# h2 doubled by TensorE instead of by DMA, 128-partition moves of states and index keys, and tile 0 first in the opening

## The chip, the cores and the metric

The kernel runs on one core of one Trainium2 chip. The metric is the device time of one launch in microseconds; the median of several launches is quoted.

## What is computed

One step of a streaming encoder layer on 384 tokens of width 1024: 256 prompt tokens and 8 streams of 16 tokens. It is cut here to what matters.

```python
h = rmsnorm(x, ln1_g); q_a, k_a, v_a, q_i, k_i, w_i, q_b, k_b, v_b, g_b = split(h @ w_in)
score = sum_h w_i * relu(q_i . k_i)          # index scores, masked by chunk
idx = top_k(score)                           # 64 of 128/256 keys, 132 of 528
o_a = softmax(q_a . k[idx]) @ v[idx]         # sparse attention
o_b, S_new = retention(q_b, k_b, v_b, S)     # 4 heads, state (64, 128) each
x = x + concat(o_a, silu(g_b) * norm(o_b)) @ w_out
h2 = rmsnorm(x, ln2_g)
q = h2 @ w_query                             # 8 heads, two halves of 128
i1, i2 = top16(q1 . keys1), top16(q2 . keys2)
e, gate = top16 of the 256 sums; gate = softmax
x = x + sum_{head, 16} gate * gelu(u[e] . h2) * v[e]     # rows of u, v: 16384 x 1024
y = rmsnorm(x, ln_final_g)
```

## The kernel before

The tokens are three tiles of 128: tiles 0 and 1 are the prompt, tile 2 is the 8 streams. Each tile has 8 experts' heads of 16 chosen experts, so there are 24 units (tile, head) and 384 steps n of one gather each. A step n belongs to unit n // 16 and to tile n // 128.

**The expert stream.** GpSimd issues the gathers: step n fetches 128 rows of 8 KB (one expert's u and v for each partition) into one of 8 row buffers, n % 8. VectorE multiplies the u half with the token's h2 and sums; ScalarE applies Gelu, multiplies with the gate and builds a diagonal matrix; TensorE (`add_experts`) takes two steps at a time with 8 matmul records of 512 columns and adds the v halves to the tile's output in PSUM. Gather n + 8 waits for `acc` of step n. Since one gather serves 64 tokens with two experts each, VectorE needs every token's h2 twice: `h2r` holds, for j = 0 and 1, the rows of h2 of half j on both halves of the partitions. In this kernel four DMAs on SyncE's queue (`twice`) copy h2 there for each tile, each from 64 partitions to 64 partitions.

**The work beside the stream.** Each engine has one instruction stream in order. From step 0 on, each engine's program holds the stream's instruction of step n, and after it those parts of the other work whose written time `until(k)` has come: queries and top-16 of the later units, the attention and retention of tiles 1 and 2, their output projections, and the index scores of tile 2. These numbers k are steps.

**The opening.** Before step 0 everything that unit 0 of tile 0 needs has to be done: projections, index scores and top-64, attention, retention, output projection (`x1_done` reaches 2), the norm of h2, its transposes (`h2_t`), the query of unit 0, the scores against the expert keys (`query_scores`), `top16(0)` on VectorE, and `spread_out(0)` with `spread_take(0)`, which raises `picked` and lets the first gather go. In this kernel the opening also holds the index queries, index scores, top-64 and attention scores of tile 1 (`two_tiles`, `sums_1`, `scores_1`, `row_max`, `exps_1`, `scale_probs`), the index queries of tile 2 (`later_qi`) and the attention queries of tiles 1 and 2 (`later_qa`).

**Buffers that order the loads.** The eight row buffers hold weights at first: gathers 0 to 3 go where `w_out` of tile 0 was, gathers 4 and 5 where `w_qi` is and wait for `qi_ps` 3, gathers 6 and 7 where `w_qa` is and wait for `qa_ps` 3. Slot 0 of `wt` (named T) holds tile 1's index queries, weights and scores, and afterwards the query weights `w_q`, of which one quarter (2 MB, two units) is loaded at a time by `load_q(k)` once the units that use the quarter before are done.

**SyncE's queue** issues every other load and store in the order of the program. The states `s0` (1 MB in, 1 MB out) go in two DMAs of 64 partitions each, and the index keys `cki` in eight DMAs of 64 partitions.

Of the kernel before, what the change touches and what calls it, by code (L numbers as in the profile page):

```python
# [19 lines left out]
ALU = mybir.AluOpType  # L20
# [3 lines left out]
P = 128  # L24
D = 1024
KC = D // P
# [4 lines left out]
HI = 8  # L31
# [52 lines left out]
def build(nc, a, o):  # L84
    with ExitStack() as ctx:
# [179 lines left out]
        w_in = {n: sem("w_" + n) for n in ("kv", "qi", "qa", "vb", "qkb", "gb", "out0", "out1", "out")}  # L265
# [7 lines left out]
        h2r_in = [sem(f"h2r_in{t}") for t in range(TILES)]  # L273
# [43 lines left out]
        def q_at(u):  # L317
            return {2: 0, 3: 6, 8: 88, 16: 224, 17: 230}.get(u, 16 * u - 48)
# [40 lines left out]
        def _(sp):  # L359
# [23 lines left out]

            sp.wait_ge(kv_sb, TILES)
# [26 lines left out]
            sp.dma_start(wt[:, 4, :], a["w_out0"]).then_inc(w_in["out"], 16)  # L411
            load_q(3)
            sp.wait_ge(gb_ps, 3)
            sp.dma_start(wt[:, 5, :], a["w_out1"]).then_inc(w_in["out"], 16)
# [12 lines left out]
            for e in range(2):  # L427
                sp.dma_start(s0[64 * e:64 * e + 64, :, :, :], a["s0"][e]).then_inc(s0_in, 16)
# [4 lines left out]
            for e in range(2):  # L433
                sp.dma_start(o["state_s"][e], s0[64 * e:64 * e + 64, :, :, :]).then_inc(ss_out, 16)
# [1397 lines left out]
```

## Time and profile before

| | |
|---|---|
| median of 3 runs | 1257.58 us (1254.51 to 1259.72) |
| profiled execution, its own time | 1257.35 us |
| its span, first to last instruction | 1255.6 us |
| busy: TensorE, VectorE, ScalarE, GpSimd | 900.1, 812.7, 486.1, 436.7 us |
| moved by DMA | 463.92 MB, of it 402.68 MB by the gathers |

The span is what lies between the first and the last instruction; the profiled execution's own time is 1.75 us longer. Busy times of engines overlap, so they don't add up to the span.

### The profile page before, as it was taken

The page shows a single profiled execution, that of the slowest core. Times are in us where ns is not written, and L with a number is a line of the kernel's source. Part 1 is how long each engine was busy: PE and PEld are TensorE (multiplying, and loading weights), DVE is VectorE, ACT ScalarE, POOL GpSimd, SP SyncE. Part 2 cuts the span into 40 slices and gives each one's busy share as a digit, 9 for nine tenths or more (in the row PEclk, how much of TensorE's full clock was granted, in tenths as well). Part 3 has the DMA queues.
Part 4 walks back from the last instruction along what each step waited for, and adds up shares of the span by engine and source line. Part 5 has one row for each costly group of instructions (what it writes and reads, how often), then busy time and mean ns, then how long its engine had stood idle before and what let it go on. Part 6 is the DMA issues. An engine that isn't in the chain of part 4 may idle for free.

```text
span 1255.6 us, 12036 instructions
## 1 busy us (share of the span) xinstructions
PE 900.1 (72%) x3676; PEld 407.6 (32%) x3676; DVE 812.7 (65%) x2103; ACT 486.1 (39%) x1444; POOL 436.7 (35%) x405
## 2 busy tenths in 40 slices
PE   6999787997696875765776786746757777665564
PEld 4855643442233232332333432222222222221110
DVE  2152557585576668998676785836696776677543
ACT  2111234253344443243366664422453443444332
POOL 0000134253244342334443333523444444443440
PEclk9899988899798896978787889878787778777866
DMA  9611479999999999989999999999999999999994
GB/s 381 269 68 34 148 299 424 373 365 424 394 421 365 397 364 421 418 332 420 419 420 420 417 421 422 420 364 422 398 418 389 422 421 422 420 422 417 422 420 164
DMA packets 67793, 463.92 MB, mean 369 GB/s; under 512 B 8720, under 2 KB 10512, under 8 KB 15760
## 3 DMA queue, kind: packets, MB, share of 16 engines
q0 software_dynamic: 55296, 402.68, 78.9%
q1 hardware_dynamic: 12432, 60.47, 12.5%
q8 instruction: 29, 0.48, 0.2%
q14 instruction: 36, 0.29, 0.1%
HBM read 456.73 MB, written 3.24 MB: 366 GB/s over the span
## 4 chain that ended last, share of the span: by engine, by line
DMA 44%; PE 28%; DVE 15%; issue 5%; ACT 4%; POOL 3%; SPq 0%; DVEq 0%; POOLq 0%
DMA rows<-in_uv,ids 43%; PE ps L530 27%; DVE rows L1765 7%; POOL rows L500 3%; ACT work L1088 1%; ACT wgt L1088 1%; DMA wt<-in_w_q 1%; PE ps L533 1%; DVE wt L1377 1%; DVE top L1373 1%; ACT zact L1088 1%; ACT L1088 1%; ACT wt L1088 0%; DMA half<-in_half 0%; DVE work L1486 0%
## 5 line engine op out<-in xcount | busy, mean ns | idle before, releaser
L530 PE MATMUL ps<-rows,work 128*64 128x512 f32 x1536 | 488.1, 768 | 309.5 <-ACT work L1088 309.1
L500 POOL DMA_INDIRECT rows<-in_uv,ids x384 | 418.6, 1090 | 679.2 <-PE ps L530 585.8
L1765 DVE CUSTOM_DVE_ANT_0 rows<-rows,masks 128x1024 f32<-128x1024 f32 x256 | 313.5, 1226 | 196.6 <-DMA rows<-in_uv,ids 194.0
L1088 ACT ACTIVATE zact<-zdot 128x1 f32<-128x1 f32 x384 | 77.5, 202 | 590.0 <-DVE zdot L1765 589.4
L530 PEld LDWEIGHTS ps<-rows,work 128*64 128x64 f32 x1536 | 111.2, 162 | 581.0 <-ACT work L1088 413.1
L1765 DVE CUSTOM_DVE_ANT_0 rows<-rows,wt 128x1024 f32<-128x1024 f32 x128 | 157.1, 1227 | 100.7 <-DMA rows<-in_uv,ids 99.0
L530 PE MATMUL ps<-wt 128*128 128x512 f32 (+4 forms) x476 | 141.5, 442 | 2.9 <-DVE wt L1544 1.9
L1088 ACT ACTIVATE work<-pair,wgt 128x64 f32<-128x64 f32 x384 | 133.5, 348 | 12.5
L530 PEld LDWEIGHTS ps<-work,wt 128*128 128x128 f32 (+1 forms) x776 | 100.0, 204 | 69.1 <-issue 67.9
L530 PE MATMUL ps<-work,wt 128*128 128x128 f32 (+1 forms) x776 | 114.9, 297 | 5.3 <-DMA wt<-in_w_q 4.4
L1088 ACT ACTIVATE wgt<-zact,gates 128x1 f32<-128x1 f32 x384 | 113.1, 295 | 12.5
L530 PEld LDWEIGHTS ps<-wt 128*128 128x128 f32 (+1 forms) x476 | 73.5, 194 | 61.2 <-issue 54.9
L1088 ACT ACT_TABLE_LOAD x66 | 84.7, 1283 | 1.9 <-PEq L1815 0.7
L1088 ACT ACTIVATE wt<-ps 128x512 f32<-128x512 f32 (+5 forms) x59 | 32.2, 555 | 81.2 <-PE ps L530 55.7
L530 PE MATMUL ps<-wt,rows 128*128 128x128 f32 (+1 forms) x320 | 48.0, 314 | 0.0
L530 PEld LDWEIGHTS ps<-wt,rows 128*128 128x128 f32 x320 | 45.1, 209 | 2.7 <-issue 1.0
L1765 DVE DVE_READ_ACCUMULATOR2_ANT zdot<- 128x1 f32 x384 | 31.5, 82 | 0.0
L530 PE MATMUL ps<-wt,work 128*128 128x512 f32 x64 | 30.0, 606 | 0.0
L479 POOL TENSOR_TENSOR rstd<-veps,half 128x4 f32<-128x4 f32 x3 | 4.4, 1456 | 70.1 <-DVE veps L1427 70.0
L475 POOL TENSOR_TENSOR rstd<-ms,half 128x1 f32<-128x1 f32 x9 | 8.4, 928 | 54.9 <-DVE ms L1358 48.6
L1456 DVE MAX8 work<-ps 128x8 f32<-128x128 f32 x48 | 11.9, 290 | 19.7 <-PE ps L530 19.4
L530 PE MATMUL ps<-x,wt 64*128 64x128 f32 (+4 forms) x100 | 22.7, 346 | 2.0 <-DVE x L1552 2.0
(134 smaller groups left out, 608.8 us busy)
## 6 DMA issues: line engine op xcount, KB each, us to landing
wt<-in_w_q SPq DMA_DIRECT2D x10, 2048.0 KB, 12.5
rows<-in_uv,ids POOLq DMA_INDIRECT x384, 13.0
rows<-in_w_out SPq DMA_DIRECT2D x2, 2048.0 KB, 32.3
wt<-in_w_out SPq DMA_DIRECT2D x2, 2048.0 KB, 12.2
wt<-in_ckv SPq DMA_DIRECT2D x16, 256.0 KB, 11.4
x<-in_x SPq DMA_DIRECT2D x5, 512.0 KB, 8.7
rows<-in_w_qi SPq DMA_DIRECT2D x1, 2048.0 KB, 13.2
rows<-in_w_qa SPq DMA_DIRECT2D x1, 2048.0 KB, 15.3
```

The lines of the kernel that those rows point to most:

```text
L475: pool.tensor_tensor(rstd[:, n:n + 1], ms[:, n:n + 1], half4[:, 0:1], ALU.pow).then_inc(rsd, 1)
L479: pool.tensor_tensor(rstd4[:], veps[:], half4[:], ALU.pow).then_inc(o_rstd, 1)
L500: pool.indirect_dma_start(row[s], None, a["uv"], bass.IndirectOffsetOnAxis(ap=ids[:, own(n // KP).start + n % KP:own(n // KP).start + n % ...
L530: return nc.tensor.matmul(out, lhsT, rhs, start=start, stop=stop)
L533: return nc.tensor.transpose(out, in_, ident[0:k, 0:k])
L1088: return nc.scalar.activation(*args, **kw)
L1373: then(V.max(out=top8[:], in_=score))
L1377: then(V.match_replace(out=score, in_to_replace=top8[:], in_values=score, imm_value=TAKEN))
L1456: ins = V.max(out=top[:, e, 0:8], in_=s[e])
L1765: V.tensor_tensor_reduce(row[s][:, 0:D], row[s][:, 0:D], h2r[t % 2][:, n % 2, :], 1.0, 0.0, ALU.mult, ALU.add, zdot[:, s:s + 1]).then_inc( ...
```

## The change

`twice` is no longer a DMA. TensorE multiplies 64 rows of `pair` (a 128 x 128 matrix with a one where the two indices agree modulo 64) with 64 rows of h2, which puts those rows on both halves of the partitions in one PSUM bank; four such matmuls of 512 columns and four ScalarE copies make the `h2r` of a tile. VectorE waits for `h2r_set` in place of the DMA's semaphore. The states move in one DMA over 128 partitions each way, and the index keys in four DMAs over 128 partitions (two streams at a time); ScalarE copies the even streams' index queries to the lower partitions for it.

In the opening, tile 0's index queries go alone, tile 0's scores, retention and output come before everything of tile 1, and the index queries, scores and top-64 of tile 1 follow behind tile 0's query and its `query_scores`. Index queries of tile 2 come before the query of unit 1, the attention queries of tiles 1 and 2 are last. Attention scores, maxima, exponentials and scaling of tile 1 move from the opening to steps 0 to 14, and what follows them of tile 1's attention and retention, and the projections, comes about 2 to 8 steps later. Tile 1's index data moves out of slot 0 of `wt`, so that `load_q(0)` is issued ahead of the cache outputs; `load_q(3)` moves ahead of the `state_p` output and of `w_out`.

The diff is cut; left out are changed step numbers (most of tile 1 later by 2 to 6), bank numbers, and the order of tile 0's pieces on ScalarE.

```diff
-        T = wt[:, 0, :]
...
-        qiT1 = at(T, 0, HI * P).rearrange("p (g h t) -> p g h t", h=HI, t=STEPS)
-        wz1 = at(T, 1024, WZ)
-        relu1 = at(T, 2176, 1024).rearrange("p (b n) -> p b n", b=2)
-        score1 = at(T, 3200, 256)
+        qiT1 = at(B, 7168, HI * P).rearrange("p (g h t) -> p g h t", h=HI, t=STEPS)
+        relu1 = at(B, 5888, 1024).rearrange("p (b n) -> p b n", b=2)
+        score1 = at(B, 6912, 256)
...
+            load_q(0)
...
-            sp.wait_ge(biased, 2)
-            load_q(0)
-
-            def twice(t):
-
-                sp.wait_ge(hready, TILES + t + 1)
-                for j in range(2):
-                    for q in range(2):
-                        sp.dma_start(h2r[t % 2][64 * q:64 * q + 64, j, :], h2[64 * j:64 * j + 64, :]).then_inc(h2r_in[t], 16)
-
-            twice(0)
...
+            load_q(3)
...
-            def load_cki(b):
-                sp.dma_start(cki[64:128, b % 4, :], a["cki"][b]).then_inc(cki_in[b % 4], 16)
-
+            sp.dma_start(wt[:, 5, :], a["w_out1"]).then_inc(w_in["out3"], 16)
             sp.wait_ge(vb_sb, 3)
-            for b in range(4):
-                load_cki(b)
-            twice(1)
-            for b in range(4, STREAMS):
-                sp.wait_ge(dots, CACHE + b - 3)
-                load_cki(b)
+            for b in range(STREAMS // 2):
+                sp.dma_start(cki[:, b, :], a["cki"][2 * b:2 * b + 2].rearrange("e d t -> (e d) t")).then_inc(cki_in[b], 16)
             sp.wait_ge(summed, CACHE + STREAMS)
-            for e in range(2):
-                sp.dma_start(s0[64 * e:64 * e + 64, :, :, :], a["s0"][e]).then_inc(s0_in, 16)
+            sp.dma_start(s0, a["s0"].rearrange("e d q h v -> (e d) q h v")).then_inc(s0_in, 16)
...
-            for e in range(2):
-                sp.dma_start(o["state_s"][e], s0[64 * e:64 * e + 64, :, :, :]).then_inc(ss_out, 16)
+            sp.dma_start(o["state_s"].rearrange("e d q h v -> (e d) q h v"), s0).then_inc(ss_out, 16)
...
-            twice(2)
...
-            pool.memset(wz1, 0.0).then_inc(wz_zero, 1)
...
+            pool.wait_ge(wout, 2)
+            pool.memset(wz, 0.0).then_inc(wz_zero, 1)
...
-            def two_tiles(bank, w, j):
-
-                for t in range(2):
+            def index_queries(t, bank, j0, j1):
+
+                for j in range(j0, j1):
                     for c in range(KC):
-                        last = mm(ps[:, bank, j % 2 * 256 + t * P:j % 2 * 256 + (t + 1) * P], w[:, c, j * P:(j + 1) * P],
-                                  hT(t, c), c == 0, c == KC - 1)
-                return last
+                        last = mm(ps[:, bank, j * P:(j + 1) * P], w_qi[:, c, j * P:(j + 1) * P], hT(t, c), c == 0, c == KC - 1)
+                if j1 == 4:
+                    last.then_inc(qi_ps, 1)
 
             pe.wait_ge(w_in["qi"], 16)
-            for j in range(4):
-                if j % 2 == 0:
-                    pe.wait_ge(kv_sb, 2 + j // 2)
-                last = two_tiles(7 - j // 2, w_qi, j)
-                if j % 2:
-                    last.then_inc(qi_ps, 1)
+            index_queries(0, 4, 0, 4)
...
-            BANK1 = (0, 1, 4, 5)
-            for b in range(4):
-                for g in range(2):
-                    last = mm(ps[:, BANK1[b], g * 256:(g + 1) * 256], qiT1[0:DH, 2 * b + g, :, :], kiw[0:DH, :])
-                last.then_inc(dots, 1)
-            for j in range(2, GRP):
-                last = flipped(ps[:, 7, j * P:(j + 1) * P], w_qa, j, hT0)
-            last.then_inc(qa_ps, 1)
-            pe.wait_ge(wz_set, 2)
-
-            def sums_1(b):
-                pe.wait_ge(relued, DOTS[1] + b + 1)
-                for g in range(2):
-                    i = 2 * b + g
-                    last = mm(ps[:, 2, 0:256], wz1[:, i * P:(i + 1) * P], relu1[:, b % 2, g * 256:(g + 1) * 256], i == 0, i == 7)
-                last.then_inc(summed, 1)
-
-            sums_1(0)
-            sums_1(1)
-            pe.wait_ge(w_in["vb"], 16)
-            natural(0, w_vb, 6, 512, 0, 4)
-            sums_1(2)
-            sums_1(3)
-            natural(0, w_vb, 6, 512, 4, 8).then_inc(vb_ps, 1)
             pe.wait_ge(w_in["qkb"], 16)
...
+            def twice(t, i, bank):
+
+                j, e = divmod(i, 2)
+                r = slice(64 * j, 64 * j + 64)
+                mm(ps[:, bank, :], pair[r, :], h2[r, e * 512:(e + 1) * 512]).then_inc(dup_ps, 1)
...
+            mm(ps[:, 2, 0:P], e8[64:64 + HI, :], kiw[64:64 + HI, P:2 * P]).then_inc(w_ps, 1)
+            index_queries(1, 6, 0, 3)
+            h2_t(0)
+            index_queries(1, 6, 3, 4)
+            query(0)
+            pe.wait_ge(qi_sb, 2)
+            pe.wait_ge(wz_set, 2)
+            dots_1(0)
+            dots_1(1)
+            query_scores(0)
+            pe.wait_ge(gb_sb, 1)
+            dots_1(2)
+            dots_1(3)
+            twice(0, 0, 6)
+            sums_1(0)
+            sums_1(1)
+            twice(0, 1, 1)
+            sums_1(2)
+            sums_1(3)
+            twice(0, 2, 2)
+            twice(0, 3, 0)
+            index_queries(2, 7, 0, 1)
+            spread_out(0)
+            index_queries(2, 7, 1, 4)
+            query(1)
+            query_scores(1)
+            pe.wait_ge(h2r_set, 1)
             later_qa(0)
             later_qa(1)
-            h2_t(0)
-            query(0)
+            pe.wait_ge(qi_sb, 3)
             later_qa(2)
-            query_scores(0)
+            spread_out(1)
             later_qa(3)
-            scores_1(0)
-            query(1)
-            query_scores(1)
-            scores_1(1)
-            spread_out(0)
-            later_qi(0)
-            later_qi(1)
-            spread_out(1)
-            later_qi(2)
-            later_qi(3)
-            pe.wait_ge(qi_sb, 3)
             pe.wait_ge(qa_sb, 3)
...
-            PROJECTIONS = ((2, "qkb", 1, 3), (14, "vb", 1, 3), (20, "vb", 2, 2),
-                           (28, "gb", 1, 3), (34, "qkb", 2, 2), (42, "gb", 2, 3))
+            PROJECTIONS = ((10, "qkb", 1, 3), (20, "vb", 1, 3), (26, "vb", 2, 2),
+                           (32, "gb", 1, 3), (38, "qkb", 2, 2), (46, "gb", 2, 3))
...
+                scores_1(0)
+                yield from until(4)
+                scores_1(1)
+                yield from until(10)
                 prob_t1(0)
-                yield from until(6)
+                yield from until(14)
                 values_1(0)
                 prob_t1(1)
-                yield from until(12)
+                yield from until(20)
...
+            def twice_1():
+                for i in range(4):
+                    yield from until(84 + 4 * i)
+                    pe.wait_ge(scored, 3)
+                    if i > 0:
+                        pe.wait_ge(h2r_set, 4 + i)
+                    twice(1, i, 1)
...
+                twice(2, 0, 0)
+                twice(2, 1, 1)
+                yield
+                twice(2, 2, 2)
+                twice(2, 3, 3)
...
+            def twice(t, i, bank):
+                act.wait_ge(dup_ps, 4 * t + i + 1)
+                copy(h2r[t % 2][:, i // 2, i % 2 * 512:(i % 2 + 1) * 512], ps[:, bank, :]).then_inc(h2r_set, 1)
...
+                yield from until(7)
+                exps_1(0)
+                yield from until(11)
+                exps_1(1)
...
+                    if b % 2 == 1:
+                        yield from until(87 + 4 * (b // 2))
+                        twice(1, b // 2, 1)
...
-            dve.wait_ge(summed, DOTS[2])
-            then(V.tensor_copy(score1[:, 0:P], ps[:, 2, 0:P]))
-            then(V.tensor_tensor(score1[:, P:2 * P], ps[:, 2, P:2 * P], bar[:, 0:P], ALU.add), scored)
-            for r in range(0, TOPK[1], 8):
-                score_round(score1, r, TOPK[1], 0)
-                score_round(score1, r, TOPK[1], 1)
-            set_bias(bias1, score1)
...
+            dve.wait_ge(summed, DOTS[2])
+            then(V.tensor_copy(score1[:, 0:P], ps[:, 3, 0:P]))
+            then(V.tensor_tensor(score1[:, P:2 * P], ps[:, 3, P:2 * P], bar[:, 0:P], ALU.add), scored)
+            for r in range(0, TOPK[1], 8):
+                score_round(score1, r, TOPK[1], 0)
+                score_round(score1, r, TOPK[1], 1)
+            set_bias(bias1, score1)
...
-            row_max(1, [ps[:, b, :].rearrange("p (j n) -> p j n", j=2) for b in (1, 2)], 0, 4)
-            row_max(2, [ps[:, b, :].rearrange("p (j n) -> p j n", j=2) for b in (0, 3)], 4, 4)
...
+            def attention_1():
+                yield from until(6)
+                row_max(1, [ps[:, b, :].rearrange("p (j n) -> p j n", j=2) for b in (1, 2)], 0, 4)
+                yield from until(10)
+                scale_probs(1, prob1[:, 0, :, :], 0, 4)
+                row_max(2, [ps[:, b, :].rearrange("p (j n) -> p j n", j=2) for b in (0, 3)], 4, 4)
+                yield from until(14)
+                scale_probs(2, prob1[:, 1, :, :], 4, 4)
...
-                    dve.wait_ge(h2r_in[t], 64)
+                    dve.wait_ge(h2r_set, 4 * (t + 1))
```

## Rows read from the trace of the kernel before

**Rows 1.** page, part 2: share of busy DMA engines and GB/s, 40 slices of 31.4 us

```profile
DMA  9611479999999999989999999999999999999994
GB/s 381 269 68 34 148 299 424 373 365 424 394 421 365 397 364 421 418 332 420 419 420 420 417 421 422 420 364 422 398 418 389 422 421 422 420 422 417 422 420 164
```

**Rows 2.** timeline of GpSimd, opening: start, us, what, [idle before <-releaser]

```profile
147.85 1.14 POOL L500 DMA_INDIRECT rows<-in_uv,ids  x1 [29.61 <-DVE gates L1526]
...
167.20 1.27 POOL L500 DMA_INDIRECT rows<-in_uv,ids  x1 [14.44 <-PE ps L530]
...
173.45 1.47 POOL L500 DMA_INDIRECT rows<-in_uv,ids  x1 [1.23 <-PE ps L530]
```

**Rows 3.** timeline of TensorE, opening (records; two make one fp32 matmul)

```profile
30.93 14.45 PE L530 MATMUL ps<-wt,rows 128*128 128x128 f32 x128
...
59.42 3.72 PE L530 MATMUL ps<-x,wt 64*128 64x256 f32 x16
...
88.55 7.08 PE L530 MATMUL ps<-wt 128*128 128x512 f32 x16
...
115.19 7.07 PE L530 MATMUL ps<-wt,rows 128*128 128x256 f32 x32
...
124.03 3.81 PE L530 MATMUL ps<-work,wt 128*128 128x128 f32 x32 [0.90 <-ACT work L1088]
...
135.13 0.70 PE L530 MATMUL ps<-x,wt 64*128 64x256 f32 x2
...
160.64 0.69 PE L530 MATMUL ps<-work,pair 128*128 128x64 f32 x2 [10.10 <-DVE work L1516]
...
168.20 1.98 PE L530 MATMUL ps<-x,ident 128*128 128x512 f32 x4 [1.28 <-ACT wt L1088]
```

**Rows 4.** timeline of VectorE, opening

```profile
115.46 0.69 DVE L1443 TENSOR_TENSOR x<-ps,x 128x512 f32<-128x512 f32 x1 [2.74 <-PE ps L530]
...
131.85 0.50 DVE L1456 MAX8 work<-ps 128x8 f32<-128x128 f32 x2 [7.92 <-PE ps L530]
...
147.02 0.17 DVE L1525 CAST ids<-ps 64x16 uint32<-64x16 f32 x1 [5.22 <-PE ps L530]
...
149.11 1.29 DVE L1386 TENSOR_REDUCE rowmax<-ps 128x2 f32<-128x512 f32 x2
...
162.31 1.23 DVE L1396 TENSOR_TENSOR wt<-wt,resum 128x1024 f32<-128x1024 f32 x1
```

**Rows 5.** timeline of ScalarE, opening

```profile
60.59 0.60 ACT L1088 ACTIVATE wt<-ps 128x512 f32<-128x512 f32 x1 [8.02 <-PE ps L530]
...
168.17 1.28 ACT L1088 ACT_TABLE_LOAD   x1
169.46 0.20 ACT L1088 ACTIVATE zact<-zdot 128x1 f32<-128x1 f32 x1
```

**Rows 6.** windows: length, each engine's busy us, TensorE clock, DMA share, GB/s

```profile
45.00:59.60 14.60, 12.59 (x77) 11.65 (x76) 2.29 (x7) 2.71 (x6) 0.00 (x0) 0.77 0.48 184
340.00:380.00 40.00, 37.12 (x140) 14.97 (x139) 30.13 (x80) 17.88 (x57) 17.45 (x17) 0.96 1.01 422
310.00:340.00 30.00, 16.01 (x58) 5.96 (x57) 14.53 (x41) 10.28 (x29) 8.12 (x8) 0.77 1.01 393
380.00:412.00 32.00, 20.15 (x96) 9.39 (x96) 19.89 (x50) 13.17 (x39) 13.24 (x12) 0.89 1.02 365
412.00:440.00 28.00, 23.26 (x76) 8.06 (x76) 18.70 (x52) 11.96 (x36) 11.22 (x10) 0.88 1.02 394
457.00:480.00 23.00, 12.06 (x53) 5.76 (x53) 14.57 (x40) 5.25 (x20) 7.79 (x6) 0.78 1.02 346
811.00:835.00 24.00, 11.72 (x48) 4.95 (x48) 9.55 (x20) 6.25 (x21) 9.57 (x8) 0.79 1.02 346
180.00:235.00 55.00, 46.82 (x187) 21.27 (x186) 35.30 (x93) 23.08 (x71) 18.47 (x17) 0.88 1.01 420
235.00:300.00 65.00, 60.35 (x250) 26.60 (x252) 51.87 (x151) 29.66 (x83) 29.92 (x25) 0.97 0.96 374
```

More of the change, by code:

```diff
@@ L272, in build @@
         ckv_in = [sem(f"ckv_in{i}") for i in range(4)]
-        h2r_in = [sem(f"h2r_in{t}") for t in range(TILES)]
+        dup_ps, h2r_set = sem("dup_ps"), sem("h2r_set")
         kv_out, sp_out, ss_out, y_done = sem("kv_out"), sem("sp_out"), sem("ss_out"), sem("y_done")
@@ L596, in _ @@
                 last.then_inc(dots, 1)
-            pe.wait_ge(w_in["qa"], 16)
-            for j in range(2):
-                flipped(ps[:, 7, j * P:(j + 1) * P], w_qa, j, hT0)
+            for j in range(2, GRP):
+                last = flipped(ps[:, 7, j * P:(j + 1) * P], w_qa, j, hT0)
+            last.then_inc(qa_ps, 1)
             pe.wait_ge(wz_set, 1)
@@ L648, in _ @@
             last.then_inc(rt_ps, 1)
-            pe.wait_ge(pscaled, 1)
-            for j in range(8):
-                last = tr(psf[:, j * P:(j + 1) * P], prob0[:, j, :])
-            last.then_inc(pt_ps, 1)
+            pe.wait_ge(w_in["vb"], 16)
+            natural(0, w_vb, 6, 512).then_inc(vb_ps, 1)
             pe.wait_ge(rt_sb, 1)
@@ L657, in _ @@
             last.then_inc(s_ps, 1)
+            pe.wait_ge(pscaled, 1)
+            for j in range(8):
+                last = tr(psf[:, j * P:(j + 1) * P], prob0[:, j, :])
+            last.then_inc(pt_ps, 1)
+            pe.wait_ge(w_in["gb"], 16)
+            natural(0, w_gb, 7, 512, 0, 4)
             pe.wait_ge(pt_sb, 1)
@@ L877, in retention_1 @@
             def retention_1():
-                yield from until(16)
+                yield from until(22)
                 pe.wait_ge(rotated, 2)
@@ L882, in retention_1 @@
                 last.then_inc(rt_ps, 1)
-                yield from until(22)
+                yield from until(28)
                 pe.wait_ge(rt_sb, 2)
+                pe.wait_ge(pv_sb, 2)
                 for h in range(HB):
@@ L889, in retention_1 @@
                 last.then_inc(s_ps, 1)
-                yield from until(28)
+                yield from until(34)
                 pe.wait_ge(s_masked, 2)
@@ L904, in retention_1 @@
                 last.then_inc(sp_ps, 1)
-                yield from until(40)
+                yield from until(46)
                 mix_t(1)
             def later_out(t, per):
-                pe.wait_ge(w_in["out"], 32)
                 pe.wait_ge(mt_sb, t + 1)
@@ L1035, in index_2 @@
                 for b in range(0, STREAMS, 2):
-                    yield from until(80 + 2 * b)
+                    yield from until(82 + 2 * b)
                     if b > 0:
@@ L1041, in index_2 @@
                     dots_2(b + 1)
-                yield from until(96)
+                yield from until(98)
                 sums_2(6)
@@ L1048, in background @@
                 yield from retention_1()
-                yield from until(54)
+                yield from until(56)
                 yield from later_out(1, 3)
             def later_background():
-                yield from until(76)
+                yield from until(78)
                 h2_t(1)
@@ L1076, in later_background @@
                 h2_t(2)
-            gens = (next_spreads(), next_scores(), next_queries(), background(), later_background(), index_2(), projections())
+                yield from until(ATT2 + 78)
+                pe.wait_ge(h2t_act, 3)
+                pe.wait_ge(h2t_dve, 3)
+                twice(2, 0, 0)
[3 more added lines that the diff above has]
+                twice(2, 3, 3)
+            gens = (next_spreads(), next_scores(), next_queries(), background(), later_background(), index_2(), twice_1(), projections())
             for n in range(0, UNITS * KP, 2):
@@ L1290, in background @@
                     ins.then_inc(sp_sb, 1)
-                yield from until(45)
+                yield from until(51)
                 mix_take(1)
-                yield from until(70)
+                yield from until(72)
                 act.wait_ge(x1_done, 4)
@@ L1326, in background @@
                 h2_take(2)
+                for i in range(4):
+                    yield from until(ATT2 + 82 + i)
+                    twice(2, i, i)
             def y_square(t):
@@ L1700, in index_2 @@
                 then(V.tensor_tensor(score2[:, 512:640], ps[:, 1, 0:P], bar[:, P:2 * P], ALU.add), scored)
-                yield from until(100)
+                yield from until(102)
                 dve.wait_ge(summed, CACHE + STREAMS)
@@ L1738, in background @@
             def background():
+                yield from attention_1()
                 yield from retention_1()
```

213 lines of the change are left out of this document (110 added, 103 removed).

## The prediction, made before the changed kernel was run

> **What bounds the kernel now.** I read the page's slices first. From about 180 us to the end nearly every slice shows the DMA engines 0.9 busy or more at some 420 GB/s [rows 1]; the gathers alone are 402.68 MB (the table of the section on the profile), which at 420 GB/s is 959 us of the 1255.6. So the kernel is a DMA stream with an opening in front of it. Two things can shorten it: starting the stream earlier, and taking DMA time out of the stream. I then read the opening engine by engine. GpSimd issues gather 0 at 147.85, stands until 167.20 for gather 4, and issues gather 8, the first that waits for `acc`, at 173.45 [rows 2]. TensorE is busy for nearly all of the opening; its one long hole is 10.10 us before the spread of unit 1 at 160.64, where it waits for VectorE's top-16 [rows 3]. Last I cut the stream into windows and looked where the share is full but the rate is not: 393, 365, 394, 346 and 346 GB/s against 422 in an undisturbed stretch [rows 6]. These five windows are where the 64-partition transfers run: index keys, h2 of tile 1, index keys, states, h2 of tile 2. Neighbouring windows hold full 128-partition loads of 2 MB at 420.
>
> The sum is made against the profiled execution's own time, 1257.35 us, which is 0.23 below the median; no correction is made for that.
>
> **Term 1: up to tile 0's output.** Before, `x1_done` reaches 2 at 116.15 (115.46 + 0.69) [rows 4]. Ahead of it TensorE now does not have: tile 1's half of the index queries, 14.45 / 2 = 7.2 us; tile 1's dots, 3.7 (the 3.72 row); its weighted sums, as many columns again, 3.7 [rows 3]. That is 14.6. The window 45 to 59.6 has 2.0 us of idle TensorE and a granted clock of 0.77 [rows 6]: it waits there for VectorE's copies and then runs partly at the lower level. In the new order attention queries fill that hole. At full clock the 12.6 busy us would be some 10; I take back 4 of the 4.6. Output at 116.15 - 14.6 - 4 = 97.5. VectorE's top-64 of tile 1 also leaves, but lies beside TensorE's work; it costs nothing before and gives nothing.
>
> **Term 2: from there to gather 0.** Before this takes 147.85 - 116.15 = 31.7. On the path lie the norm, `h2_t`, the query, the scores, VectorE's top-16 from 131.85 on and then a wait of 5.22 at 147.02 for TensorE, which comes late to the spread [rows 4]. In the new order one `later_qa` (3.6, half of 7.07) between query and scores goes, two pairs of dots (1.9) come, and the spread has only short matmuls ahead of it: I give 1.5 of the 5.22 back to a wait. That is 1.7 + 3.7 = 5.4 less, so gather 0 goes at 97.5 + 26.3 = 124, 24 us earlier.
>
> **Term 3: to gather 8, the one that counts.** Gathers 0 to 7 only fill the ring. TensorE's work from 97.5 to step 0, from the same rows [rows 3]: index queries of tiles 1 and 2, 14.45; four `later_qa` of 3.55, 14.2; two queries, 7.6; dots and sums, 7.4; four doubling matmuls of 512 columns, 8 of which take 7.08, so 3.5; scores, spreads and transposes, about 2.8; `y_start`, 2.0. Together 52, and 2.5 for short waits on PSUM copies: 152. Behind the last `later_qa` ScalarE copies (0.7), loads Gelu's table (1.28 [rows 5]) and weighs two steps (1.7); before, the table load at 168.17 stood 5.3 ahead of gather 8. With the table load at about 149.5 gather 8 goes at 154.5, against 173.45: 19 us earlier. VectorE's top-64 of tile 1 (9 us) now stands between `spread_take(0)` at 123 and `top16(1)`; it is done by 132, when TensorE brings unit 1's scores, so it is hidden; without that cover it would cost its 9. The doubling's four ScalarE copies of 0.60 lie beside matmuls, and the first gathers' 10 us of transfer cover `h2r`.
>
> **Term 4: what is put into the stream's start.** Steps 0 to 14 get the attention scores of tile 1 (8 pairs: 0.70 and 0.28 each, beginning at 135.13; 6.6 with those of the other half), two times 1.3 of maxima and 1.23 of scaling on VectorE, 5.6 with the small ones [rows 3, 4], and eight exponentials on ScalarE, with up to four table loads of 1.28. TensorE is busy 46.8 of 55 us and 60.4 of 65 there and VectorE 51.9 of 65 [rows 6], so it is not free; the projections move 8 steps back to make room, unit 4's quarter of `w_q`, which is loaded only when unit 3's query is done, gets two steps more, and the ring starts full instead of with four gathers just issued. I charge 4 of the 6.6: between 0 (the ring covers it) and 12 (both engines' work in a row). Behind the waiting instruction on each engine stands the stream's next step, which GpSimd's next gather waits for; that is how it would reach the time. Front in sum: 19 - 4 = 15.
>
> The Trainium skill (ScalarE: Activation LUTs, "What ACT_TABLE_LOAD costs") gives 1.283 us for a load and 1.38 for a drain with it. Here the load at 168.17 is followed by Gelu at 169.46, so no drain is seen; with it, four loads would hold ScalarE 5.5 us longer and term 4 would be nearer 7.
>
> **Term 5: DMA time in the stream.** The shortfall of a window is its length times (1 - rate / 421). Index keys: 30 x 0.067 = 2.0 and 28 x 0.064 = 1.8. States in: 23 x 0.178 = 4.1. h2 of tile 1: 32 x 0.133 = 4.3; of tile 2: 24 x 0.178 = 4.3. The doubled h2 itself, 4 x 256 KB a tile, also goes: 1.05 MB / 421 = 2.5 each, 5 for the two in the stream. (Tile 0's ran ahead of gather 0, beside TensorE's work, and gives nothing.) Sum 21.5. The states out fall in a stretch where VectorE sets the pace; nothing is taken. I take 19: keys and states still have to move, other loads share those windows, and the doubling adds 3.5 us of TensorE to steps 84 to 96 and again behind step 228. The first place is well filled (37.1 of 40 busy just before [rows 6]), so up to 2 may come back there. Lower bound 13, if half of the shortfall has another cause; upper 21.5.
>
> The Trainium skill (SBUF — State Buffer, "Door 1: The DMA port swizzle") says that partitions 0 to 63 reach 8 of 16 ports, and a range of 128 all. The trace agrees in kind: full share, lower rate. By that rule each of four megabytes costs 2.5 us more than needed, which with the 5 of bytes gives 15 instead of 21.5.
>
> **Sum.** 1257.35 - 15 - 19 = 1223.4; I say 1223. About 0.5%, 6 us, is what a measurement of this kernel can tell from no change.
>
> **Rivals.** *The front is swallowed.* The stream's start is bound by TensorE and VectorE rather than by the ring: the 19 us stay in the first 60 steps, and TensorE, at 60.4 of 65 [rows 6], shows it. For it: the fill. Against: 8 us of idle TensorE in 180 to 235. Time: 1257.35 - 3 - 19 = 1235, or with 13 for the DMA, 1241. *The DMA's full rate is not regained*, the windows being slow for the mixture of packets: 1257.35 - 15 - 5 (bytes) = 1237. *More than forecast.* Gathers 4 to 7 are 10 us of transfer and start at 167.20 [rows 2], so at 173.45 about 4 us of them are still to come; afterwards none are. That is worth 4 to 6 us of stream. If besides term 4 is nothing and term 5 whole: 1257.35 - 24.5 - 21.5 = 1211. *No change:* the stream's pace is set elsewhere, and each microsecond gained is a wait at a later load. The full shares of rows 1 speak against it. *Slower.* TensorE falls to its lower level in the first 60 steps: the new mixture of short matmuls with waits on ScalarE's exponentials leaves gaps, and behind gaps the clock has been low (0.77 in 45 to 59.6 and in 310 to 340, where it is idle, 0.97 where it is busy [rows 6]). The 107 busy us of 180 to 300 would double at worst; it decides from where more than 34 us are added, a third of that work at the lower level. That TensorE is fuller than before speaks against it.
>
> **Chances.** Forecast (1213 to 1231) 0.55; front swallowed or rate not regained (1231 to 1245) 0.20; more than forecast (below 1213) 0.17; within 0.5% 0.04, slower 0.04. The range must leave out no more than 0.2: 1205 to 1243. Faster by over 0.5%: 0.92.
>
> **What would show it.** `x1_done` 2 near 97, gather 0 near 124, gather 8 near 154.5; no hole of 10 us before unit 1's spread; all stream windows near 420 except where loads end; the DMA total down by 3.1 MB. Term 4 is wrong if DMA's share between 155 and 280 falls under 0.93. The prediction is wrong altogether if gather 8 is early but the stream's last gather gains less than half of what it should, 34 us.

## The result and the profile after

| | before | after |
|---|---|---|
| median of 4 runs each | 1258.11 us (1254.51 to 1259.72) | 1209.85 us (1207.74 to 1211.85) |
| profiled execution, its own time | 1257.35 us | 1207.74 us |
| its span | 1255.6 us | 1205.9 us |
| moved by DMA | 463.92 MB | 460.77 MB |

The ratio is 0.962, with a 95% interval of 0.959 to 0.965: 48 us faster. Forecast were 1223 (1205 to 1243), 34 faster. The sign and the range hold, the size was 13 us short: 1209.85 lies outside the inner band of 1213 to 1231, which had a chance of 0.55, and in "more than forecast", which had 0.17. Of all launches quoted in this document one ran in the chip's slower state, 1301.39 us at a granted clock of 0.73 (a launch of before_q18); no ratio contains it.

The page's slices, DMA share and GB/s (31.4 us each before [rows 1], 30.1 now):

```profile
DMA  9800899999999999899999999999999999999994
GB/s 380 367 1 1 319 365 401 421 420 424 418 421 421 420 421 420 300 416 417 421 420 417 419 421 423 423 417 412 411 390 420 422 420 421 421 420 414 423 421 174
```

The stream begins a slice earlier, and most of the dips to 364 to 398 are gone; one of 300 is left, in a stretch where VectorE sets the pace. GpSimd's timeline in the opening answers to [rows 2]:

```profile
121.31 1.14 POOL L478 DMA_INDIRECT rows<-in_uv,ids  x1 [24.54 <-DVE gates L1546]
...
126.53 0.95 POOL L478 DMA_INDIRECT rows<-in_uv,ids  x1 [0.30 <-PE ps L508]
...
145.56 1.23 POOL L478 DMA_INDIRECT rows<-in_uv,ids  x1 [16.82 <-PE ps L508]
...
151.28 1.85 POOL L478 DMA_INDIRECT rows<-in_uv,ids  x1 [2.20 <-PE ps L508]
```

These are gathers 0, 4, 6 and 8. Gather 0 goes 26.5 us earlier, gather 8 22.2 earlier. TensorE and VectorE show why ([rows 3, 4] before):

```profile
93.98 0.69 DVE L1463 TENSOR_TENSOR x<-ps,x 128x512 f32<-128x512 f32 x1 [2.74 <-PE ps L508]
...
108.74 0.50 DVE L1476 MAX8 work<-ps 128x8 f32<-128x128 f32 x2 [7.23 <-PE ps L508]
...
120.49 0.17 DVE L1545 CAST ids<-ps 64x16 uint32<-64x16 f32 x1 [1.79 <-PE ps L508]
...
131.33 0.50 DVE L1476 MAX8 work<-ps 128x8 f32<-128x128 f32 x2 [1.47 <-PE ps L508]
```
```profile
131.06 10.53 PE L508 MATMUL ps<-wt,rows 128*128 128x256 f32 x48
141.42 0.36 PE L508 MATMUL ps<-work,pair 128*128 128x64 f32 x2
141.62 3.67 PE L508 MATMUL ps<-wt,rows 128*128 128x256 f32 x16
146.04 1.98 PE L508 MATMUL ps<-x,ident 128*128 128x512 f32 x4 [0.75 <-ACT wt L1090]
149.06 1.94 PE L508 MATMUL ps<-rows,work 128*64 128x512 f32 x8 [1.04 <-ACT work L1090]
```

Tile 0's output is there at 94.67. The attention queries (10.53) stand where the wait of 10.10 for unit 1's top-16 was, and the spread at 141.42 begins without a wait.

Differences of whole kernels hide where time comes from, so I lined up the gathers by number. Time at which the kernel before issues a gather, minus the time at which the changed one does:

| gather | 0 | 8 | 28 | 56 | 80 | 104 | 112 | 128 | 224 | 240 | 383 |
|---|---|---|---|---|---|---|---|---|---|---|---|
| earlier by, us | 26.5 | 22.2 | 28.6 | 30.9 | 29.6 | 38.4 | 43.1 | 41.4 | 40.9 | 47.7 | 47.9 |

It grows at four places: 8 to 28 (the stream's start), 80 to 104 (h2 of tile 1 and the second half of the index keys), 104 to 112 (states), 224 to 240 (h2 of tile 2). The remaining 1.7 of the 49.6 us of span comes after the last gather and is this execution's own: from there to the end it takes 25.7 us and the kernel before 27.4, but another execution of the same changed program (after_again, below) takes 27.4 too. Windows between gathers 0, 8, 28, 48 and 80, before and after (columns as in [rows 6]):

```profile
147.85:173.45 25.60, 13.18 (x74) 10.11 (x73) 20.52 (x62) 9.67 (x33) 8.11 (x9) 0.80 0.65 240
173.45:235.24 61.79, 53.61 (x237) 26.41 (x236) 37.19 (x97) 24.36 (x76) 22.41 (x21) 0.89 1.01 416
235.24:292.25 57.01, 54.48 (x230) 24.46 (x228) 44.32 (x131) 23.92 (x71) 25.66 (x21) 0.97 0.95 367
292.25:385.56 93.31, 70.44 (x261) 27.89 (x262) 59.02 (x162) 37.31 (x110) 36.37 (x34) 0.91 1.01 413
```
```profile
121.31:151.28 29.97, 27.01 (x158) 22.05 (x157) 24.91 (x83) 8.87 (x27) 9.12 (x9) 1.00 0.83 328
151.28:206.64 55.36, 48.01 (x225) 23.34 (x224) 39.04 (x100) 29.82 (x86) 23.44 (x20) 0.94 0.95 380
206.64:264.69 58.05, 58.05 (x254) 27.17 (x253) 44.72 (x130) 27.30 (x79) 24.91 (x21) 1.00 1.01 420
264.69:355.97 91.28, 72.84 (x274) 29.71 (x273) 60.29 (x167) 36.48 (x108) 37.12 (x34) 0.93 1.01 421
```

Between gathers 8 and 28 the changed kernel needs 6.4 us less although its DMA engines are the less busy ones (0.95, 380 GB/s): it has less to move there, 21.0 MB against 25.7 (rate times length), and something other than DMA sets its pace.

### The profile page after: what moved, and what is told of

It reads as the page before. It is cut to its first block, busy times and chain, and to the rows that moved or that the text cites. A ratio compares the mean times of both kernels' runs of the same rounds, so it can differ in the third digit from the quotient of the medians.

```text
span 1205.9 us, 12084 instructions
## 1 busy us (share of the span) xinstructions
PE 885.4 (73%) x3702; PEld 400.8 (33%) x3702; DVE 811.9 (67%) x2103; ACT 497.6 (41%) x1458; POOL 446.9 (37%) x405
## 2 busy tenths in 40 slices
DMA packets 66737, 460.77 MB, mean 382 GB/s; under 512 B 8432, under 2 KB 10224, under 8 KB 14704
## 4 chain that ended last, share of the span: by engine, by line
DMA 40%; PE 32%; DVE 14%; issue 6%; ACT 5%; POOL 3%; SPq 0%; POOLq 0%; DVEq 0%
DMA rows<-in_uv,ids 40%; PE ps L508 31%; DVE rows L1793 7%; POOL rows L478 3%; ACT work L1090 1%; ACT wgt L1090 1%; ACT L1090 1%; PE ps L511 1%; DVE wt L1397 1%; DVE top L1393 1%; ACT zact L1090 1%; DMA half<-in_half 0%; DVE rowmax L1406 0%; ACT wt L1090 0%; DVE work L1506 0%
## 5 line engine op out<-in xcount | busy, mean ns | idle before, releaser
L508 PE MATMUL ps<-rows,work 128*64 128x512 f32 x1536 | 471.4, 745 | 293.5 <-ACT work L1090 291.0
L478 POOL DMA_INDIRECT rows<-in_uv,ids x384 | 429.0, 1117 | 641.7 <-PE ps L508 554.4
L508 PEld LDWEIGHTS ps<-rows,work 128*64 128x64 f32 x1536 | 108.4, 158 | 564.6 <-ACT work L1090 401.7
L508 PE MATMUL ps<-wt 128*128 128x512 f32 (+4 forms) x476 | 138.2, 444 | 2.9 <-DVE wt L1564 1.9
L1090 ACT ACT_TABLE_LOAD x70 | 89.8, 1283 | 1.9 <-PEq L1843 0.7
L508 PE MATMUL ps<-wt,rows 128*128 128x128 f32 (+1 forms) x320 | 44.3, 297 | 0.0
L508 PEld LDWEIGHTS ps<-wt,rows 128*128 128x128 f32 x320 | 41.2, 192 | 2.7 <-issue 0.8
L1090 ACT ACTIVATE work<-ps 128x256 f32<-128x256 f32 (+2 forms) x49 | 16.9, 345 | 37.7 <-PE ps L508 18.8
L508 PE MATMUL ps<-work,pair 128*128 128x64 f32 (+1 forms) x72 | 24.2, 429 | 0.0
L508 PEld LDWEIGHTS ps<-keysT,work 128*128 128x128 f32 x96 | 14.5, 217 | 25.4 <-issue 25.4
## 6 DMA issues: line engine op xcount, KB each, us to landing
wt<-in_w_q SPq DMA_DIRECT2D x10, 2048.0 KB, 13.6
wt<-in_w_out SPq DMA_DIRECT2D x2, 2048.0 KB, 11.4
```

The costliest lines, as they stand in the source:

```text
L478: pool.indirect_dma_start(row[s], None, a["uv"], bass.IndirectOffsetOnAxis(ap=ids[:, own(n // KP).start + n % KP:own(n // KP).start + n % ...
L508: return nc.tensor.matmul(out, lhsT, rhs, start=start, stop=stop)
L1090: return nc.scalar.activation(*args, **kw)
```

## Experiments

Each computes the whole reference; nothing is left out. "Back" means that the piece is as in the kernel before.

**twice_dma, keys64, states64, order_only.** The changed kernel with h2 of tiles 1 and 2 copied by DMA again; with the index keys in eight 64-partition DMAs; with the states in 64-partition DMAs; and with all three back, so that only the order of the opening and the step numbers are changed. The fence shows the edits of the keys, the states and h2 of tile 2, from different runs; tile 1's h2 is handled alike, and tile 0's stays on TensorE in all of them.

```diff
-                sp.dma_start(cki[:, b, :], a["cki"][2 * b:2 * b + 2].rearrange("e d t -> (e d) t")).then_inc(cki_in[b], 16)
+                sp.dma_start(cki[64:128, b % 4, :], a["cki"][b]).then_inc(cki_in[b % 4], 16)
...
-            sp.dma_start(s0, a["s0"].rearrange("e d q h v -> (e d) q h v")).then_inc(s0_in, 16)
+            for e in range(2):
+                sp.dma_start(s0[64 * e:64 * e + 64, :, :, :], a["s0"][e]).then_inc(s0_in, 16)
...
-                twice(2, 0, 0)
-                twice(2, 1, 1)
...
+                    sp.dma_start(h2r[2 % 2][64 * q:64 * q + 64, j, :], h2[64 * j:64 * j + 64, :]).then_inc(h2r_in[2], 16)
```

> The changed kernel (1209.9 us) with h2 of tiles 1 and 2 doubled by four 64-partition DMAs again; tile 0's stays on TensorE. Theory A (term 5 as forecast: 5.0 us of bytes and 8.6 us of lost rate, both on the path): 1209.9 + 13.6 = 1223.5, and the windows in which the copies run fall from 420 to about 350 GB/s. Rival B (the slow windows had another cause, only the bytes count): 1215. Rival C (TensorE's and ScalarE's doubling costs the stream as much as it saves): 1210.

> The changed kernel with the index keys in eight DMAs of 64 partitions again, nothing else changed. Theory A (64 partitions lower the rate): 3.8 us more, 1213.7. Rival B (the keys' windows were slow because of the h2 copies and w_out beside them): 1210.

> The changed kernel with the states in and out in two DMAs of 64 partitions each again. Theory A: 4.1 us more, all of it kept to the end: 1214. Rival B: the rate is lost as in A, but the stretch behind it, where VectorE is 19.4 of 20 us busy, is no DMA stretch and takes part of it back: gather 104 later by 4, the end by 1 to 3: 1211 to 1213.

> The changed kernel with all three DMA parts undone (h2 of tiles 1 and 2, keys, states), so the opening's order and the step numbers alone, beside the kernel before. Theory A (terms add up, front worth 29 us, DMA parts 19): 1258.1 - 29 = 1229. Rival B (front worth the 15 forecast, DMA parts worth 33 because they relieve more than their windows): 1243.

| | median us | ratio to before | profile against the changed one's |
|---|---|---|---|
| twice_dma | 1220.55 (1216.76 to 1224.92) | 0.972 [0.9692, 0.9748] | last gather 7.3 later |
| keys64 | 1215.04 (1211.4 to 1215.88) | 0.9657 [0.9629, 0.9685] | 6.8 later at gather 104, 1.3 at the last |
| states64 | 1214.56 (1213.06 to 1215.56) | 0.9661 [0.9636, 0.9686] | 4.5 later at gather 112, 3.9 at the last |
| order_only | 1227.15 (1226.14 to 1230.39) | 0.9768 [0.9741, 0.9795] | last gather 17.5 later |

(The last column is the time at which a gather is issued, later than in the changed kernel. For keys64 and states64, whose openings ran 4.3 and 3.9 us late, that is taken off; the last section tells of it.) Windows of the transfers, of twice_dma, then keys64, then states64:

```profile
364.00:390.00 26.00, 16.39 (x70) 6.30 (x72) 14.73 (x40) 7.73 (x26) 9.11 (x9) 0.81 1.02 362
774.00:800.00 26.00, 12.40 (x48) 5.51 (x48) 8.64 (x19) 5.66 (x19) 9.70 (x8) 0.80 1.02 357
```
```profile
302.00:325.00 23.00, 14.94 (x55) 5.84 (x52) 11.68 (x31) 10.59 (x23) 7.77 (x8) 0.85 1.02 386
385.00:410.00 25.00, 25.00 (x70) 8.13 (x68) 17.23 (x45) 11.57 (x33) 8.92 (x8) 0.71 1.02 391
```
```profile
426.00:450.00 24.00, 14.08 (x53) 5.25 (x51) 15.19 (x42) 5.83 (x20) 7.05 (x7) 0.79 1.02 359
```

The changed kernel in the two stretches of the first fence, then its control (after_again, whose opening is late by as much as those of keys64 and states64) in the three others:

```profile
364.00:390.00 26.00, 20.48 (x82) 7.44 (x82) 19.73 (x52) 11.03 (x36) 11.29 (x10) 0.82 1.01 422
774.00:800.00 26.00, 16.37 (x76) 7.56 (x74) 10.71 (x18) 7.17 (x24) 8.81 (x9) 0.76 1.01 421
```
```profile
302.00:325.00 23.00, 15.27 (x55) 5.98 (x52) 11.79 (x32) 11.49 (x27) 9.09 (x8) 0.78 1.02 419
385.00:410.00 25.00, 21.41 (x96) 8.97 (x96) 18.67 (x49) 14.54 (x41) 11.55 (x11) 1.00 1.01 420
426.00:450.00 24.00, 12.83 (x57) 5.41 (x55) 17.19 (x46) 6.47 (x23) 8.88 (x8) 0.78 1.01 420
```

The share is full in all of them, the rate is not: each kind of 64-partition transfer lowers it, and each brings its dip back alone. The rival "rate not regained" falls, and with it the mixture of packets as the cause: states64 has the changed kernel's bytes and 32 packets more of 66737.

The length of the stream from gather 80 to gather 383 is a steadier measure than the end, since the openings' scatter is not in it:

| us | gather 8 to 80 | gather 80 to 383 |
|---|---|---|
| changed kernel, after_again, after_q16, maxima_8, ring_late | 204.0 to 205.1 | 822.6 to 824.9 |
| att_open | 199.8 | 822.4 |
| keys64 | 205.0 | 825.9 |
| states64 | 204.7 | 828.8 |
| twice_dma | 204.0 | 832.9 |
| order_only | 204.4 | 842.5 |
| before | 212.1 | 842.6 |
| before_q18, before_spread | 205.1, 204.8 | 842.0, 843.4 |

Against the mean of the first row, 823.5, the h2 copies cost 9.4 us, the states 5.3 and the keys 2.4, with a scatter of about 1; all three at once, which is order_only and the kernel before, cost 19. The dip of the first index keys lies before gather 80 and delays nothing up to there. The keys' 6.8 at gather 104 is not all DMA: in the window from 385 their TensorE is busy for all 25.00 us at a granted clock of 0.71, where the control has 21.41 and 1.00, and most of the delay is gone at the last gather.

By ratio, against the control's 0.963 (a later comparison, on another chip), the three alone cost 11, 3 and 4 us, together 18 to 19, and all three at once 17. Each of these differences has an interval of some 5 us either way, so the times alone show the h2 copies and the three together, but not keys or states by themselves. Against what was expected: the copies cost 11 timed, between theory A's 13.6 and rival B's 5; states64 goes with theory A, with the delay between gathers 104 and 112; keys64's windows are A's, its end in the trace is between the two. What is left, the order alone, is 0.9768, 29 us (26 to 33); theory A of order_only said 29.

**ring_late.** Are gathers 4 and 5, which the changed order lets go 20 us before gather 8, what is behind the extra? They are made to wait for the last attention query, as 6 and 7 do.

```diff
                 if n == 4:
-                    pool.wait_ge(qi_ps, 3)
+                    pool.wait_ge(qa_ps, 3)
```

> The changed kernel with gathers 4 and 5 held until the last attention query is done, as 6 and 7 are, so 4 gathers instead of 6 run before the rest; gather 8 is issued when it was. Theory A (what counts is how many gathers the DMA has moved, not when gather 8 is issued): two gathers of 2.5 us are moved later, 5 us slower, 1215, with gather 8 within 1 us of 151.3. Rival B (gather 8 counts, as my term 3 had it): 1210.

1212.4 us (1209.83 to 1212.71), ratio 0.966 [0.9639, 0.968]. Its window from gather 8 to gather 28:

```profile
154.20:208.94 54.74, 47.04 (x225) 22.52 (x224) 40.86 (x103) 30.21 (x88) 21.91 (x21) 0.97 1.01 420
```

The backlog is there, 2.0 MB more at 420 instead of 380 GB/s, and in the trace it costs nothing: 54.7 us against 55.4, and 205.1 against 204.7 up to gather 80. In the changed kernel the ring is not what counts in this stretch; the engines are. The times are less clear. The median lies between the two theories, and against the control's 0.963 the ratio is 3.8 us worse, with an interval of nearly 5 either way; they exclude neither.

**att_open.** The attention scores, maxima, exponentials and scaling of tile 1 go back into the opening, behind `later_qa(3)`.

```diff
             later_qa(3)
             pe.wait_ge(qa_sb, 3)
+            scores_1(0)
+            scores_1(1)
...
-                scores_1(0)
-                yield from until(4)
-                scores_1(1)
```

> The changed kernel with tile 1's attention scores, maxima, exponentials and scaling at the end of the opening again instead of in steps 0 to 14. Gather 8 goes some 10 to 14 us later (6.6 on TensorE, then maxima, exponentials and scaling in a row). Theory A (in the stream this work costs next to nothing): 8 to 12 us slower, 1218 to 1222. Rival B (my term 4: in the stream it costs 4 and more, so much of it is only moved): 3 to 6 us slower, 1213 to 1216.

1221.19 us (1220.35 to 1225.48), ratio 0.9746 [0.9724, 0.9769]: 11 to 15 us slower than the changed kernel (0.966 and 0.963 are the two ratios to set it against: ring_late's on the same chip, and the control's below). Gather 8 and the window from it to gather 28:

```profile
168.95 1.59 POOL L478 DMA_INDIRECT rows<-in_uv,ids  x1 [21.09 <-PE ps L508]
```
```profile
168.95:219.08 50.13, 41.21 (x201) 20.02 (x200) 32.52 (x90) 20.30 (x64) 22.27 (x20) 0.93 0.96 395
```

In the opening this work holds gather 8 back by 17.7 us, where 10 to 14 were expected; in steps 0 to 14 it costs 55.4 - 50.1 = 5.3. So the total is theory A's, or more, and its reason is not: the work does cost 4 and more in the stream, as rival B had it, but the opening would pay over three times that.

**before_spread and before_q18.** The kernel before with the changed kernel's step numbers for everything behind tile 1's attention scores; and with only one of them, unit 4's query two steps later.

```diff
-            return {2: 0, 3: 6, 8: 88, 16: 224, 17: 230}.get(u, 16 * u - 48)
+            return {2: 0, 3: 6, 4: 18, 8: 88, 16: 224, 17: 230}.get(u, 16 * u - 48)
```

> The kernel before, its opening and its DMAs unchanged, with only the step numbers of the change behind step 14: projections, retention and output of tile 1 two to six steps later, unit 4's query at 18 in place of 16, and w_q's fourth quarter loaded before w_out. It asks where the 7.3 us of DMA time went that the kernel before loses between 235 and 292 us and the changed one does not. Theory A (that stretch was overfull, spreading empties it): 4 to 7 us faster, 1252. Rival B (it was filled by the work that was late from a late start, the step numbers do nothing): 1258.

> The kernel before with unit 4's query at step 18 instead of 16, nothing else; all the later step numbers together made it 2.6 to 3.6 us faster. Theory A (the w_q wait): the same 3 us, TensorE's wait of 4.4 us at 217 gone. Rival B: 0 to 1 us.

before_spread: 1251.64 us (12 runs, 1246.7 to 1255.87), ratio 0.9971 [0.9952, 0.999]. before_q18: 1251.75 (12 runs, 11 of them 1247.21 to 1256.73), ratio 0.9974 [0.9951, 0.9998]. TensorE's waits from 145 to 300 us, of the kernel before and of before_q18 (us in total, times, longest):

```profile
PE ps L530 <- DVE work L1516: 10.1, 1, 10.1
PE ps L530 <- ACT work L1088: 9.5, 5, 3.8
PE ps L530 <- DMA wt<-in_w_q: 4.4, 1, 4.4
PE ps L530 <- ACT wt L1088: 1.3, 1, 1.3
```
```profile
PE ps L530 <- ACT work L1088: 12.4, 7, 3.5
PE ps L530 <- DVE work L1516: 10.1, 1, 10.1
PE ps L530 <- ACT wt L1088: 1.3, 1, 1.3
```

and before_q18 from gather 8 to 28 and from there to gather 48:

```profile
172.81:228.30 55.49, 50.18 (x229) 23.81 (x228) 35.23 (x93) 22.23 (x70) 20.84 (x21) 0.94 1.01 420
228.30:284.82 56.52, 53.76 (x238) 25.11 (x236) 46.78 (x135) 25.90 (x77) 26.30 (x22) 1.00 1.01 415
```

One number removes the wait of 4.4 and takes 6.3 us off the stretch (61.8 to 55.5); up to gather 80 it is 7.0 (212.1 to 205.1), and before_spread has 7.3. By the timed runs it is 3.3 us with an interval of 0.3 to 6.2, and for before_spread 3.6 with 1.3 to 6.0, so the profiles' 6 to 7 are at the upper edge or over it. The profiled launches are part of the reason: before_q18's, at 1247.40, is 4 us faster than its median, and 1257.35 is 2 slower than the median of the kernel before in this comparison (1255.23). The other step numbers add nothing that can be measured: both ratios are the same.

**after_again, after_q16, maxima_8.** The changed kernel unchanged, as the control; with unit 4's query back at step 16; and with the second half's row maxima at step 8 ahead of the first half's scaling at 10, since TensorE waits 4.94 us for `work` there.

```diff
-            return {2: 0, 3: 6, 4: 18, 8: 88, 16: 224, 17: 230}.get(u, 16 * u - 48)
+            return {2: 0, 3: 6, 8: 88, 16: 224, 17: 230}.get(u, 16 * u - 48)
...
+                yield from until(8)
+                row_max(2, [ps[:, b, :].rearrange("p (j n) -> p j n", j=2) for b in (0, 3)], 4, 4)
                 yield from until(10)
                 scale_probs(1, prob1[:, 0, :, :], 0, 4)
-                row_max(2, [ps[:, b, :].rearrange("p (j n) -> p j n", j=2) for b in (0, 3)], 4, 4)
```

> The changed kernel itself, as a control beside the three others. Both theories: ratio to the kernel before 0.962 again.

> The changed kernel with unit 4's query at step 16 again instead of 18, nothing else. Theory A (the wait for w_q's second quarter is what the early stream gains from the new step numbers): TensorE waits there again, 3 to 5 us slower, 1213 to 1215. Rival B (the gain comes from the projections and the retention lying later, not from this wait): within 1 us of the control.

> The changed kernel with the second half's row maxima of tile 1 at step 8 instead of in one go with the scaling at step 10, where TensorE waits 4.94 us and then runs at the lower clock level. Theory A (that pile is what the early stream still loses): 2 to 3 us faster than the control. Rival B (the pile is only moved, unit 2's top-16 stands beside it at either step): no difference.

after_again 1211.32 us (1207.14 to 1212.7), ratio 0.963 [0.9599, 0.9662]; after_q16 1211.76 (1208.64 to 1215.04), 0.9638 [0.9607, 0.9669]; maxima_8 1207.54 (7 runs, 1205.95 to 1214.73), 0.9603 [0.9573, 0.9632].

after_q16 costs nothing that shows: 204.0 us from gather 8 to 80, and 1.0 us by ratio, with an interval of over 5 either way that by itself does not exclude theory A's 3 to 5. The wait doesn't come back, because the quarter is no longer late: the kernel before issues its load at 209.66 and comes to the query at 217.04, 7.4 us later, and waits until 221.44; after_q16 issues it at 193.68 and comes to the query at 203.49, 9.8 later, with nothing in front of TensorE. The kernel before, then after_q16:

```profile
209.66 0.33 SPq L382 DMA_DIRECT2D wt<-in_w_q  x1
...
221.44 2.04 PE L530 MATMUL ps<-work,wt 128*128 128x128 f32 x8 [4.40 <-DMA wt<-in_w_q]
```
```profile
193.68 0.33 SPq L380 DMA_DIRECT2D wt<-in_w_q  x1
...
203.49 1.16 PE L508 MATMUL ps<-work,wt 128*128 128x128 f32 x8
```

So the wait is removed twice over in the changed kernel: either the rest of the change or the two steps alone does it. maxima_8 has the lowest median measured, but its interval and the control's overlap; it is not shown to be faster.

## Why the prediction came out as it did

**What bounds it:** right. From gather 28 to 80 the stream runs at 420 to 421 GB/s with a full share; from 8 to 28 it does not (0.95, 380).

**Term 1** (`x1_done` at 97.5): 94.67, 2.8 earlier. **Term 2** (26.3 from there): 26.6; gather 0 at 121.31 for a forecast of 124. The top-64 of tile 1 ends at 129.9 and unit 1's scores come at 131.33: hidden, as forecast. **Term 3** (gather 8, 19 earlier): 22.2 earlier, 151.28 for 154.5; the three came with term 1. They are no larger than the scatter of one program's opening: the control has gather 0 at 124.98 and gather 8 at 155.15, 18.3 earlier than before. So terms 1 to 3 were right within what one profile can tell. The opening without the table load's supposed tail is right too: the load at 146.00 lasts 1.28 and Gelu follows at 147.30, as in [rows 5]:

```profile
146.00 1.28 ACT L1090 ACT_TABLE_LOAD   x1
147.30 0.20 ACT L1090 ACTIVATE zact<-zdot 128x1 f32<-128x1 f32 x1
```

The Trainium skill (ScalarE: Activation LUTs, "What ACT_TABLE_LOAD costs") has the 1.283 us right: the 70 loads take 1283 ns each in the mean. Its drain of 1.38 doesn't appear here either. Four more loads in the whole kernel, 66 to 70, as said.

**Term 5** (DMA time in the stream, 19): 18.3 from gather 80 on in the profiled execution, 19.9 in the control. By ratio it is 17 together and 18 to 19 as the sum of three. The total was right; the pieces were less so. The h2 copies were to cost 13.6 and cost 9.4 to 11, the states 4.1 and cost 4 to 5, the keys 3.8 and cost 2 to 3. Their traces add up to 17.1 where the working had 21.5, and the 2.5 taken off it brought the forecast near.

The rule of the Trainium skill (SBUF — State Buffer, "Door 1: The DMA port swizzle") agrees in kind with every window above, a full share at a lower rate; the ports themselves are not seen in a trace. The estimate of 15 in sum that the prediction worked out from it would have been 3 to 5 too low by the traces.

**Term 4 is the step that failed.** It reads "I charge 4 of the 6.6", and with it "Front in sum: 19 - 4 = 15". From gather 8 to gather 80 the change was to lose 4 us and it gained 7.4 (212.1 to 204.7). The charge itself was about right: the moved attention costs 5.3 in the stream (att_open). What the step left out was on the other side of the sum, and it had named both items in its own sentence without giving them a price:

- "unit 4's quarter of `w_q` ... gets two steps more": the wait of 4.4 us at 217 held up gather 28 by 6.3 (before_q18, in the trace; 3.3 timed). I had read the window 235 to 300 with its share of 0.96 and 374 GB/s [rows 6] only as a sign that TensorE is full. But from gather 28 to 48 the kernel before moves 367 GB/s, 7.3 us short of 421 over 57.0 us; before_q18 moves 415 there. So something in the kernel before was to be had.
- "the ring starts full": with the wait gone, the kernel before is still DMA-bound from gather 8 to 28 (55.5 us at a full share, 23.3 MB), with gathers 4 to 7 and loads in arrears. The changed kernel without attention there needs 50.1 us. These 5.4 I put down to the full ring and the earlier loads; they are read from two different kernels and not from one with only the ring changed, so this cause is not shown. The attention's 5.3 use them up.

The stretch then takes the same with both: 55.5 us in before_q18, bound by bytes, and 55.4 in the changed kernel, bound by its engines. The 6.3, 5.4 and 5.3 are steps between four kernels in a row (61.8, 55.5, 50.1, 55.4), so that they add up to the 6.4 of the table is no test of them. The test is before_q18 alone: one changed number brings the kernel before from 212.1 us to 205.1, where all versions of the changed kernel with the attention in the stream are.

The profiled execution is 49.6 us faster than before's, 15.6 more than forecast: 3.2 by term 3, 11.4 by term 4 (7.4 gained for 4 lost), 1.7 behind the last gather, less 0.7 by term 5. The control is 45.8 faster, 11.8 more than forecast, and term 4 is nearly all of it: 18.3 at gather 8, 7.6 up to gather 80, 19.9 from there and nothing behind. The size rests on one profile of the kernel before; if the timed 3.3 is the truer worth of the wait, 3 to 4 us of the shortfall stay unexplained.

**The rivals.** *Front swallowed* is refuted: the gain grows from 22.2 us at gather 8 to 29.6 at gather 80 (18.3 to 25.9 in the control). *Rate not regained* is refuted by the windows. *More than forecast*, given 0.17 and 1211 us, is nearest to the number, and that is partly luck: its ring's credit, if the 5.4 is that, doesn't add to a term 4 of nothing but pays for the attention, and in ring_late's trace another 2 MB of arrears costs nothing. What carried the time down there, the wait for `w_q`, stood in no rival. *Slower*: the granted clock from gather 8 on is 0.94, 1.00 and 0.93 where it was 0.89, 0.97 and 0.91, so it did not fall. The share under 0.93 between 155 and 280 that was to show term 4 wrong did not come (0.95 and 1.01 in the two windows there): that test looked for a loss only.

The change is two changes: the order is worth 29 us (order_only), the transfers 17 to 20.

## What to carry to other kernels

Before charging a stretch for the work put into it, look whether the stretch is losing time already (a DMA share under full, a single wait for a load): a change that shifts a query by two steps can give that back (here 3 us timed, 6 to 7 in the trace), and it belongs in the sum as a term. Where a stretch is bound by bytes in one version and by engines in the other, its time is the larger of the two, and what is taken from the smaller gives nothing. Line kernels up by gather number before explaining a difference. Beside a full stream like this one, transfers should span all 128 partitions, and a copy for which TensorE and ScalarE have room shouldn't be a DMA (9.4 to 11 us here for the h2 of two tiles).

## What the hardware showed unexpectedly

The same program's opening differs by 3.7 us between executions, in a stretch where TensorE never stands still. From 60 to 90 us of the changed kernel and of its control:

```profile
60.00:90.00 30.00, 30.00 (x102) 14.81 (x102) 7.62 (x22) 8.26 (x24) 1.02 (x1) 1.00 0.00 1
```
```profile
60.00:90.00 30.00, 30.00 (x95) 15.10 (x96) 8.12 (x24) 8.26 (x24) 1.02 (x1) 0.89 0.00 1
```

The granted clock is 1.00 in one and 0.89 in the other, so part of the stretch ran at the lower of the two levels (1.2 and 2.4 GHz), with TensorE busy for 30.00 of 30.00 us in both. The records show it so; the ends of matmuls are modelled in them. Gather 0 goes at 121.31 and at 124.98. Of the eleven profiles of the experiments six show 0.89 there, one 0.95 and four 1.00; what brings it about, the runs don't show. Of the changed kernel's four times two are 1207.74 and 1208.11 and two 1211.59 and 1211.85; the first, profiled, had 1.00 in that stretch. That this clock makes the two groups would fit but is not shown: the other three have no profile. Two kernels 3 us apart can't be told apart by one profile each.

The second thing is the rate under a full share. 64-partition transfers beside the gathers leave the DMA engines as busy as before (1.02) and move 357 to 391 GB/s in place of 419 to 422; over the windows above that is 26 x (1 - 362 / 421) = 3.6 us for the copies of one h2 (4.0 for the other), 24 x (1 - 359 / 421) = 3.5 for a megabyte of states, and 1.9 and 1.8 for the two halves of the keys. A share alone doesn't show it; the rate beside it does.
